# Each dense matmul of 512 tokens issued as two of 256 tokens, with the weights loaded for each

## What is computed

```
h  = rms_norm(x, g);  z = h @ w_in                       # 1024 -> 18..34 tiles of 128
x  = x + merged @ w_out
x  = x + square(relu(rms_norm(x) @ w_up)) @ w_down       # first block
x  = x + 0.5 * (silu(h @ w_gate) * (h @ w_up)) @ w_down  # four times
x  = x + concat(attention, convolution) @ w_out          # twice
```

## Time and profile before

| | |
|---|---|
| Median of 2 runs | 2605.28 us (2604.14 to 2606.43) |
| Profiled execution, its own time | 2604.31 us |
| Its span, from first to last instruction | 2602.5 us |
| Mean granted TensorE clock | 0.995 of full speed |
| TensorE matmuls and weight loads | 11494 and 11494 |
| DMA, mean over the span | 90 GB/s |

### The profile page before, as it was taken

How to read it: one execution, slowest core, us unless ns; L and a number is a source line. 1 busy time by engine, 2 the same in 40 slices (tenths; PEclk the granted TensorE clock), 3 DMA queues, 4 the chain that set the end, 5 groups by cost and what they waited for, 6 DMA issues and landing times.

```text
span 2602.5 us, 28067 instructions
## 1 busy us (share of the span) xinstructions
PE 2567.8 (99%) x11494; PEld 2079.9 (80%) x11494; DVE 1232.8 (47%) x1518; ACT 886.6 (34%) x1329; POOL 276.8 (11%) x194
## 2 busy tenths in 40 slices
PE   8999999999999999999999999999999999999997
PEld 6777888888888888877888888888888778888885
DVE  5444455344465343455454444543434645544444
ACT  4445434223343222344332222422223443322222
POOL 4233110000020000013300000100000132000002
PEclk9999999999999999999999999999999999999998
DMA  6111232333223333231223332333332312332332
GB/s 161 49 49 53 89 115 92 97 97 97 91 88 105 97 96 92 84 104 57 75 96 99 96 97 92 95 97 97 98 97 81 100 61 77 95 100 90 98 92 69
DMA packets 69423, 235.36 MB, mean 90 GB/s; under 512 B 8752, under 2 KB 11440, under 8 KB 69296
## 3 DMA queue, kind: packets, MB, share of 16 engines
q1 hardware_dynamic: 67632, 230.36, 28.6%
q0 software_dynamic: 1664, 3.22, 0.7%
HBM read 231.35 MB, written 2.19 MB: 90 GB/s over the span
## 4 chain that ended last, share of the span: by engine, by line
PE 92%; DVE 4%; ACT 2%; issue 1%; DMA 0%; POOL 0%; SPq 0%; DVEq 0%; ACTq 0%
PE bank L756 29%; PE bank L758 28%; PE bank L757 28%; PE bank L770 2%; PE bank L797 2%; DVE w_lo L1064 1%; PE bank L784 1%; ACT w_hi L868 1%; DVE x L1165 1%; ACT z L859 0%; DVE q L1121 0%; DVE z L1056 0%; PE bank L808 0%; DMA w_raw<-w_in_dram 0%; PE bank L830 0%
## 5 line engine op out<-in xcount | busy, mean ns | idle before, releaser
L756 PE MATMUL bank<-h_hi,w_hi 128*128 128x512 f32 x2224 | 892.0, 401 | 9.4 <-DVE w_lo L1064 9.4
L758 PE MATMUL bank<-h_hi,w_lo 128*128 128x512 f32 x2224 | 869.4, 391 | 0.0
L757 PE MATMUL bank<-h_lo,w_hi 128*128 128x512 f32 x2224 | 868.8, 391 | 0.0
L1064 DVE TENSOR_TENSOR w_lo<-w_raw,w_hi 128x1024 fp32r<-128x1024 f32 (+1 forms) x387 | 483.9, 1252 | 329.4 <-ACT w_hi L868 329.0
L868 ACT ACTIVATE w_hi<-w_raw 128x1024 fp32r<-128x1024 f32 (+1 forms) x438 | 452.0, 1034 | 431.0 <-PE bank L758 428.4
L756 PEld LDWEIGHTS bank<-h_hi,w_hi 128*128 128x128 f32 x2224 | 418.8, 188 | 108.3 <-DVE w_lo L1064 10.9
L758 PEld LDWEIGHTS bank<-h_hi,w_lo 128*128 128x128 f32 x2224 | 418.8, 188 | 88.5
L757 PEld LDWEIGHTS bank<-h_lo,w_hi 128*128 128x128 f32 x2224 | 419.4, 189 | 81.9 <-issue 1.9
L758 PE MATMUL bank<-act_hi,w_lo 128*128 128x512 f32 x960 | 379.2, 395 | 0.0
L756 PE MATMUL bank<-act_hi,w_hi 128*128 128x512 f32 x960 | 379.2, 395 | 0.0
L757 PE MATMUL bank<-act_lo,w_hi 128*128 128x512 f32 x960 | 379.1, 395 | 0.0
(11 more groups left out here) (163 smaller groups left out, 1669.9 us busy)
## 6 DMA issues: line engine op xcount, KB each, us to landing
w_raw<-ffn_wg_dram SPq DMA_DIRECT2D x88, 512.0 KB, 3.5
w_raw<-ffn_wu_dram SPq DMA_DIRECT2D x88, 512.0 KB, 3.5
w_raw<-w_in_dram SPq DMA_DIRECT2D x70, 512.0 KB, 3.5
w_raw<-ffn_wd_dram SPq DMA_DIRECT2D x64, 512.0 KB, 3.5
w_raw<-w_up_dram SPq DMA_DIRECT2D x32, 512.0 KB, 3.5
w_raw<-w_down_dram SPq DMA_DIRECT2D x32, 512.0 KB, 3.8
w_raw<-w_out_dram SPq DMA_DIRECT2D x24, 512.0 KB, 3.5
w_raw<-ffn_wd_dram SPq DMA_DIRECT2D x32, 384.0 KB, 3.1
```

Source lines behind the costliest of these rows:

```text
L756: engine.matmul(to, w_hi[s][:, lhs], hi, start=k == 0, stop=False)
L757: engine.matmul(to, w_hi[s][:, lhs], lo, start=False, stop=False)
L758: product = engine.matmul(to, w_lo[s][:, lhs], hi, start=False, stop=job == "k_last")
L1064: engine.tensor_tensor(lo, value, hi.bitcast(F32), ALU.subtract).then_inc(signals[event].s, 1)
```

## The change

Inside a dense step, each of the three matmuls of 512 tokens becomes two of 256 tokens, the first on tokens 0 to 255 and the second on tokens 256 to 511, each with its own call of `engine.matmul`, and so with its own load of the same 128x128 weights. Both halves write their half of the same PSUM bank. The order of the three products stays. `start` is set only on the first half of the first product of a result. The increment of `mm_done` is put on the last half of the last product. Nothing else is touched.

```
-                    engine.matmul(to, w_hi[s][:, lhs], hi, start=k == 0, stop=False)
-                    engine.matmul(to, w_hi[s][:, lhs], lo, start=False, stop=False)
-                    product = engine.matmul(to, w_lo[s][:, lhs], hi, start=False, stop=job == "k_last")
+                    for n, (w, a) in enumerate(((w_hi[s], hi), (w_hi[s], lo), (w_lo[s], hi))):
+                        for tokens in (slice(0, TOKENS // 2), slice(TOKENS // 2, TOKENS)):
+                            product = engine.matmul(to[:, tokens], w[:, lhs], a[:, tokens], start=k == 0 and n == 0 and tokens.start == 0,
+                                                    stop=job == "k_last" and n == 2, skip_group_check=True)
```

## The result

The changed kernel takes 2690.72 us (median of 2 runs, 2690.02 to 2691.43) against 2605.28 before. The ratio is 1.033, with a 95% interval from 1.0305 to 1.0355. The forecast was 2625 us, at most 2% from before: the time is inside the range of 2590 to 2775 us, but 85 us were added where 20 were forecast, so the case that came is a slower one.

What follows compares the result with a forecast made beforehand. The prediction took TensorE's distance between matmuls as the bound: 13 us with h and 7 us with the other operands, 20 us on 2604.3, gave 2624.3, and 1.0 us to the median made 2625 us; range 2590 to 2775 us.

Steps and rivals of the forecast that it cites:

- The bound: Whole kernel: TensorE, busy 99% of the span, almost never waits, so the distance between matmuls goes into the time in full.
- The stream: Dense matmuls: the extra 13.8 or 19.7 ns over 213.3 looks like a rate per column, so splitting adds little.
- The rival: Hand-over between weights inside TensorE: the extra is paid per matmul, 164 us more, 2769 us; chance 0.15.
- the rivals: Alternatives on dense-step pacing: three slower, chance 0.36 together, and one faster, 0.05; the range reaches over the first two slower.
- The clue at 1.2 GHz: First matmuls at the lower clock: starts 0.42 us apart are the bare stream, so the extra isn't always there.
- The triple of scores: Score matmuls of 256 columns, 64 active rows, own loads: 115 ns each, taken as nearest to the new dense step.
- The others: Dense matmuls with operands other than h: 235.0 against 233.0 ns per pair, 2.0 ns x 3648 = 7 us.
- The load: Weight load beside a half: about 110 ns, still hidden by a stream of 113.5 or 116.5 ns.
- The rival in which the load is the bound: Dense halves: a load of 120 ns sets the pace, 240 per pair, 112 us more, 2717 us; chance 0.13.
- The instruction supply: TensorE's sequencer: at 126 ns per half, 235 us more, 2840 us; a rival with chance 0.08.
- a sign that the load or the supply is the bound: Changed profile's dense halves: the same distance between starts for both kinds of operand would show one of these limits.
- What a measurement can tell: Whole-kernel time: a difference of 2% or less (52 us) can hardly be told from no change.

Runs made afterwards that it cites:

- e2: Changed kernel with each dense matmul split into 320 and 192 tokens in place of two of 256: 2891.83 us, ratio 1.110.
- e12: Changed kernel, moving tiles on multiples of 512 bytes, one 320-token matmul replacing the halves (rest left out) except in each result's first product: 1971.18 us, ratio 0.758.
- e1: Changed kernel with each dense matmul split into 384 and 128 tokens in place of two of 256: 3175.24 us, ratio 1.218.
- e11: Changed kernel, moving tiles on multiples of 512 bytes, one 384-token matmul replacing the halves (rest left out) except in each result's first product: 2144.84 us, ratio 0.824.
- e9: Changed kernel, halves kept, moving tiles on multiples of 512 bytes, 72 of 128 weight columns in all but each result's first product: 2662.56 us, ratio 1.023.
- e5: Kernel before, two small tiles moved away so that all moving tiles begin on a multiple of 512 bytes: 2588.68 us, ratio 0.992.
- e15: Kernel before, moving tiles other than h placed 256 bytes past a multiple of 512 in place of 128: 2587.75 us, ratio 0.993.
- e16: Kernel before, moving tiles other than h placed 64 bytes past a multiple of 512 in place of 128: 2594.29 us, ratio 0.995.
- e10: Whole 512-token matmuls, moving tiles on multiples of 512 bytes, 72 of 128 weight columns in all but each result's first product: 2611.74 us, ratio 1.003.

## Why the prediction was wrong

**The bound, right.** TensorE sets the time, the other engines only gained slack, and the sum of distances between starts accounts for 87.0 of 87.1 us. The counts of the page (21814 and 21814) are as foretold, and the 2.82 MB of instructions, the waits (8.7 us for `w_lo`) and the granted clock (0.997) show no new limit.

**The stream, wrong, and this is the step that failed**: "So the extra looks like a rate per column, about 58.3 ns per 128 for these operands and 56.8 for `h`". For `h`, two thirds of the matmuls, the extra is 13.3 ns per matmul at every length tried (256, 320, 384 and 512 columns), and the split pays it twice. The forecast had 1.9 ns x 6672 = 13 us there; measured were 13.3 ns in the steady stages and 72.7 us in all. The rival priced it at 13.8 x 6672 = 92 us. That the time fell inside the range is no merit of the forecast: the range was drawn wide enough for the rivals.

How the reading went astray can be said exactly. The earlier trace rows hold only tiles that lie off the multiple of 256 bytes, where the distance really grows faster with the length (114.6 ns from 256 to 512 columns, and I read 116). They said nothing on `h`; the 56.8 came from dividing the 227.1 of the earlier trace rows by its own length, which assumes what was to be shown. That the two kinds differ was noted as an argument for the rival ("it differs by operand, which a fixed rate doesn't explain by itself") and then not followed: a view of two kinds with different behaviour is a warning not to carry the line of one to the other. The clue at 1.2 GHz, 0.42 us for 512 columns with no extra to be seen, was noted and not followed either.

**The triple of scores, used too widely.** Its 115 ns per 256 columns is a single triple read to 10 ns, off the multiple too, with 64 rows. Off the multiple single halves lie anywhere between 115 and 122 ns, so one triple cannot give their mean: it is 118.7, and 120.0 for `h`.

**The others, small as foretold, but twice the size.** 2.0 ns x 3648 = 7 us were forecast, 4 ns and 15.1 us measured. The rival's 19.7 x 3648 = 72 us was wrong here: most of the extra of these tiles at 512 columns goes with the length. So neither case came whole; the rival was right on `h`, and on the rest the forecast was the nearer. 13.3 ns x 6672 = 89 and 15 make 104 us, of which 16 with `h` were not paid: the attention stages, the clock and the shorter waits. The prediction had put nothing on any of the three.

**The load, right.** It was put at 110 ns and hidden by 113.5; it is 110.0 (e2 with e12) to 113.5 ns (e1 with e11) beside a stream, hidden by 120. The Trainium skill (TensorE: Matmul & The Clock Gate, section "LDWEIGHTS (loading the stationary operand)") gives columns / 1.2 GHz, 107 ns for 128. The traces have 3 to 7 ns more. The rival in which the load is the bound fell with e9: with loads of 72 columns the halves went to 118.3 and not to 113.3 ns.

**The instruction supply, right to be doubted.** Starts are 120.0 ns apart in halves with full loads, and the second part of e2 takes 110.0, so two instructions per 110 ns are no limit. The near equality of the two kinds, 120.0 and 118.7, was named as a sign that the load or the supply is the bound; it was not one, because the lines of the two kinds lie that close together at 256 columns.

The Trainium skill (the same page, section "Back-to-back issue gap") gives columns / 2.4 GHz plus a constant of 2.5 ns for matmuls in isolation. On the multiple the traces here have that form; with a load for each matmul, in `fp32r`, the constant is 13.3 ns.

**What a measurement can tell, wrong.** The prediction counted a difference of up to 2% as hardly to be told from no change. The interval of the ratio here is a quarter of a per cent to either side, so even the 0.8% of the forecast would have been clear of it.

What stays open: whether the 13.3 ns belong to the matmul or to the change of weights. In this kernel every matmul comes with its own load, so halves that share one load were not tried. Whether the loaded weights are new or the same again makes no difference: both kinds of step are 120.0 ns here with `h`. Nor is it known why a whole matmul is 3.9 ns longer and a half 1.7 ns shorter with loads of 72 columns, or by what mechanism an address 128 bytes past a multiple of 256 makes the long stream slower and the half faster.

## What to carry to other kernels

Before pricing a split, measure the same operation at two lengths in the same steady state and of the same operands: a fixed part and a rate look alike at one length, and are told apart by a second. Count a cost per instruction against the number of instructions; 13 ns are hard to see in a duration of 400, and 73 us in this kernel. Where two groups of equal shape run at different distances, look at the addresses of their operands: shifting some tiles by 128 bytes was worth 0.8% here (e5), where the split cost 3.3%.

## What the runs showed of the hardware that was not expected

- `fp32r` matmuls of 128x128 weights, each with its load, at 2.4 GHz, moving tile on a multiple of 512 bytes: 226.7, 173.5, 146.7 and 120.0 ns between starts for 512, 384, 320 and 256 columns. At 1.2 GHz it is 0.42 us for 512 and 0.43 for two halves, without the extra.
- The same with the moving tile 128 bytes past: 233.3, 176.0, 146.8 and 118.7 ns. 256 bytes past (e15) is as good as the multiple for 512 columns, 226.7 ns; at 64 bytes past (e16) it is 228.9 ns. In the time of the whole kernel, e16 is 0.2 to 0.3% behind e5 and e15, and the kernel before 0.8%.
- With loads and outputs of 72 columns in place of 128, 512-column streams were slower, 230.6 in place of 226.7 ns (e10).
- Two loads of 128 columns start 108 ns apart at the least, two of 72 columns 61 ns (e9).
